# Last block of a fused four-block kernel: eight steps of one head pair regrouped into four steps of two pairs

## The reference

```python
h = _rmsnorm(x, norm_g) * (1 + scale) + shift
c_val, c_gate, c_og, ts, r_og, g_conv, g_rwkv = split(h @ w_in)
# convolution branch: 31 causal taps on each of 1024 channels
u = layernorm(causal_conv(c_val * sigmoid(c_gate), conv_k) + conv_b)
y_conv = (silu(u) * silu(c_og)) @ w_conv_out
# recurrent branch: 16 heads of 64, one state of 64x64 for each head
r, k, v, w_low, a_low = split(ts + mu * (previous(ts) - ts))
for t in tokens:
    sk = state @ kk[t]
    state = state * w[t] - outer(sk, b[t]) + outer(v[t], k[t])
    o[t] = state @ r[t]
o = layernorm_per_head(o) + sum(r * k * r_k) * v
y_rwkv = (o * silu(r_og)) @ w_rwkv_out
m = sigmoid(g_conv) * y_conv + sigmoid(g_rwkv) * y_rwkv
x = x + gate * (m @ w_out);  return _rmsnorm(x, final_g)
```

## Time and profile before

| | us |
|---|---|
| median of 3 runs (1036.30 to 1037.82) | 1036.68 |
| the profiled execution's own time | 1036.78 |
| its span, first to last instruction | 1035.0 |
| TensorE busy in the span | 1002.3 (97%) |
| VectorE busy | 869.7 (84%) |
| ScalarE busy | 604.3 (58%) |

### The profile page before, as it was taken

The page is one execution under the profiler, slowest core; times in us unless marked ns, Lnnn a source line. Parts: engine busy times, 40 slices in busy tenths (PEclk is TensorE's granted clock), DMA queues, the critical chain, the costliest instruction groups (busy, mean ns, idle before and its releaser), DMA issues.

```text
span 1035.0 us, 25000 instructions
## 1 busy us (share of the span) xinstructions
PE 1002.3 (97%) x10690; PEld 932.6 (90%) x10690; DVE 869.7 (84%) x1447; ACT 604.3 (58%) x875; POOL 18.4 (2%) x38
## 2 busy tenths in 40 slices
PE   7999999999999999999999999999999999899997
PEld 6999999999999989989898998889999998789996
DVE  7866699899988886999899897989999999965474
ACT  7755664444446756554444577556657676686443
POOL 2000000000000000000000000000000000000000
PEclk9999999999999999999999999999999999999999
DMA  9662457777554515576775646334323422234531
GB/s 283 214 203 94 152 189 252 230 243 227 199 176 149 164 47 181 200 231 227 241 234 182 203 133 194 109 99 124 122 86 123 125 84 84 84 124 155 170 126 41
DMA packets 136075, 168.26 MB, mean 163 GB/s; under 512 B 3216, under 2 KB 125328, under 8 KB 135728
## 3 DMA queue, kind: packets, MB, share of 16 engines
q1 hardware_dynamic: 132080, 153.44, 46.1%
q0 software_dynamic: 3904, 13.50, 4.0%
HBM read 164.83 MB, written 2.10 MB: 161 GB/s over the span
## 4 chain that ended last, share of the span: by engine, by line
PE 68%; DVE 22%; ACT 6%; issue 2%; DMA 2%; SPq 0%; DVEq 0%; ACTq 0%
PE banks L353 13%; PE banks L318 8%; PE banks L319 7%; PE banks L320 7%; PE banks L355 7%; DVE hf L2652 4%; DVE w_parts L304 3%; DVE w_parts L280 3%; PE banks L655 2%; PE bank L657 2%; PE bank L655 2%; PE banks L657 2%; PE bank L659 2%; PE banks L659 2%; ACT w_parts L275 1%
## 5 line engine op out<-in xcount | busy, mean ns | idle before, releaser
L280 DVE TENSOR_TENSOR w_parts<-raw,w_parts 128x2048 fp32r<-128x2048 f32 x95 | 217.1, 2288 | 27.3 <-ACT w_parts L275 26.8
L353 PE MATMUL banks<-x_parts,w_parts 128*128 128x512 f32 x640 | 227.1, 399 | 0.0
L318 PE MATMUL banks<-x_parts,w_parts 128*128 128x256 f32 x704 | 211.9, 301 | 0.0
L319 PE MATMUL banks<-x_parts,w_parts 128*128 128x256 f32 x736 | 208.3, 283 | 0.0
L320 PE MATMUL banks<-x_parts,w_parts 128*128 128x256 f32 x704 | 199.1, 283 | 0.0
L275 ACT ACTIVATE w_parts<-raw 128x2048 fp32r<-128x2048 f32 x95 | 180.9, 1905 | 3.6 <-PE banks L810 2.1
L355 PE MATMUL banks<-x_parts,w_parts 128*128 128x256 f32 x640 | 179.8, 281 | 0.0
L353 PEld LDWEIGHTS banks<-x_parts,w_parts 128*128 128x128 f32 x640 | 120.3, 188 | 29.0
L319 PEld LDWEIGHTS banks<-x_parts,w_parts 128*128 128x128 f32 x736 | 141.2, 192 | 0.5 <-issue 0.5
L318 PEld LDWEIGHTS banks<-x_parts,w_parts 128*128 128x128 f32 x704 | 134.5, 191 | 7.6 <-issue 0.7
L320 PEld LDWEIGHTS banks<-x_parts,w_parts 128*128 128x128 f32 x704 | 134.8, 192 | 0.0
(11 more groups left out here) (418 smaller groups left out, 2411.6 us busy)
## 6 DMA issues: line engine op xcount, KB each, us to landing
raw<-in_ffn_w_up SPq DMA_DIRECT2D x44, 1024.0 KB, 5.1
raw<-in_w_in SPq DMA_DIRECT2D x36, 1024.0 KB, 5.5
raw<-in_ffn_w_down SPq DMA_DIRECT2D x22, 1024.0 KB, 5.9
big<-in_ada_w_t POOLq DMA_DIRECT2D x24, 512.0 KB, 4.1
raw<-in_gla_w_in SPq DMA_DIRECT2D x11, 1024.0 KB, 5.6
raw<-in_attn_w_qkv SPq DMA_DIRECT2D x6, 1024.0 KB, 4.9
raw<-in_gla_w_out SPq DMA_DIRECT2D x4, 1024.0 KB, 5.5
raw<-in_attn_w_out SPq DMA_DIRECT2D x4, 1024.0 KB, 4.9
```

The costliest lines, as they stand in the source:

```text
L280: eng.tensor_tensor(WL[:, n % RING, :, :], RAW[:, n % RING, :, :], WH[:, n % RING, :, :].bitcast(F32), ALU.subtract).then_inc(w_lo_ready, 1)
L318: nc.tensor.matmul(ps, wh, xh, start=start, stop=False)
L319: nc.tensor.matmul(ps, wh, xl, start=False, stop=False)
L353: nc.tensor.matmul(PS[bank + m].rearrange("p (a t) -> p a t", a=2), WH[:, s, k, ms], XP[:, :, k, :], start=k == 0, stop=False, skip_group_ ...
```

## The change

**Steps of two pairs.** There are now four "duos" of two pairs, and steps -2 to 4 with 13 slots each. Step `s` does the chain of duo `s`, the inverse of duo `s+1`, the fronts of the two pairs of duo `s+2`, and the norms of duo `s-1`. Slots 0 to 2 of the inverse are `scores` and `turned_keys` of the first pair, those of the second pair, and the `seeds`. Slots 3, 5, ..., 11 are `y_part`, slots 4, 6, ..., 12 are `x_part`. Each handles eight chunk parts instead of four, so that VectorE's mask is one operation of 128x512 in place of two of 128x256, and ScalarE's copy is 128x1024 in place of two of 128x512. The chain's copies are 128 wide in place of 64. The number of small matmuls does not change.

**The fronts.** The first pair's front keeps slots 0 to 6, the second pair's goes through slots 6 to 11: ScalarE scales the keys and takes the first sigmoid in slot 6, TensorE sums them in slot 7, VectorE keeps the sums in slot 7, TensorE and ScalarE form the second sigmoid in slot 8, VectorE mixes the keys in slot 8, TensorE sums in slot 9, and so on.

**Remainders in place.** The tiles for two pairs take 24 tiles, for which the remainder part of `w_parts` is used. From the fourth block of the last part to `rout0` the remainder is written over the raw weights (`LO_IN_RAW`), so a load into that slot waits for the matmuls of the block there (`block_done`) and not for its remainder.

**Splits.** The high halves of a block are formed at the last unit of the block two before it and at the first unit of the block before it; the low halves at units 2 and 4 of the block before it.

**Blocks and taps.** Block table as in the diff: 4, 5, 6, 6, 5, 9 blocks in steps -2 to 3, then `cout2`, `cout3` and the last eight. The taps are spread over 114 half slots: the last five slots of step -2 and all of steps -1 to 2. The layer norm of the convolution is in slots 0 to 3 of step 3.

**The end.** `rout_part` is gone. `rout0` is an ordinary block that waits for all pairs in turn (`rwkv_split`). The norms of the last duo are in slots 0 to 2 of step 4, beside `cout2` and `cout3`. The order of splits and mixes on ScalarE and VectorE in the last eight blocks is changed a little.

```diff
 STEP_BLOCKS = {
     -3: _blocks("r0 k0 v0"),
-    -2: _blocks("val0 gate0"),
-    -1: _blocks("r1 k1 v1 val1"),
-    0: _blocks("gate1 val2 rog0 gate2"),
-    1: _blocks("r2 k2 v2 val3"),
-    2: _blocks("gate3 rog1 gr0 gr1"),
-    3: _blocks("r3 k3 v3 gr2"),
-    4: _blocks("rog2 gr3 gc0"),
-    5: _blocks("gc1 gc2"),
-    6: _blocks("rog3 og0 og1 og2 og3"),
-    7: _blocks("gc3 cout0 cout1 cout2 cout3"),
-    8: _blocks("rout0 rout1 rout2 rout3 out0 out1 out2 out3"),
+    -2: _blocks("val0 gate0 k1 r1"),
+    -1: _blocks("v1 val1 gate1 k2 r2"),
+    0: _blocks("v2 val2 gate2 k3 r3 gc0"),
+    1: _blocks("rog0 v3 val3 gate3 gr0 gc1"),
+    2: _blocks("rog1 gr1 gr2 gr3 gc2"),
+    3: _blocks("rog2 gc3 og0 og1 og2 og3 rog3 cout0 cout1"),
+    4: _blocks("cout2 cout3 rout0 rout1 rout2 rout3 out0 out1 out2 out3"),
+DUOS, SLOTS = 4, 13
+LO_IN_RAW = range(N_L3 + 3, N_ROUT + 1)
...
+        def w_lo(n):
+            return (RAW_LO if n in LO_IN_RAW else WL)[:, n % RING, :, :]
...
         def load(sp, n, src, i=0):
-            if n >= RING:
+            if n - RING in LO_IN_RAW:
+                sp.wait_ge(block_done, n - RING + 1)
+            elif n >= RING:
                 sp.wait_ge(w_lo_ready, n - RING + 1 + RING * i)
...
                 for u in range(8):
                     q = (8 * b + u) * last // per
                     put_at(s, q, ("unit", n, u))
-                    if u % 2 == 0:
-                        put_at(s, q, ("hi" if u < 4 else "lo", n + 2, u // 2 % 2))
+                    if u == 0 and n > N_L3 + 3:
+                        put_at(s, q, ("hi", n + 1, 1))
+                    if u in (2, 4) and n > N_L3 + 3:
+                        put_at(s, q, ("lo", n + 1, u // 2 - 1))
+                    if u == 7:
+                        put_at(s, q, ("hi", n + 2, 0))
...
-        TAP_FIRST, TAP_SLOTS = 4, 20 + 6 * 24
+        TAP_FIRST, TAP_SLOTS = 16, 10 + 4 * 2 * SLOTS
...
+            def later_slots(p, q, s, r):
+                if 0 <= p < DUOS:
+                    chain_hop(p, r)
+                for i, (e, c) in enumerate(PARTS):
+                    if 0 <= p < DUOS:
+                        chain_part(p, r, i)
+                    if 0 <= q < DUOS and r % 2:
+                        y_part(q, (r - 3) // 2, e, c)
+                    elif 0 <= q < DUOS:
+                        x_part(q, (r - 4) // 2, e, c)
+                    front_pieces(s + 2, r, i)
+                    norm_pieces(s - 1, s, r, i)
...
              def kk_sums(p, c):
                 if c == 0:
                     pe.wait_ge(sem("kk_squares"), p + 1)
-                    pe.wait_ge(sem("sigmoids_ready"), p + 1)
+                    pe.wait_ge(sem("sigmoids_ready"), 2 * p + (1 if p % 2 else 2))
...
 +            def front(d, r):
...
+                elif r == 6:
+                    keys_scaled(second)
+                    decay_sigmoid(second, T)
+                elif r == 8:
+                    rate_sigmoid(second, 2, T)
+                    kk_root(second)
+                elif r == 10:
+                    decay_exps(second)
...
 +            def front(d, r):
...
+                elif r == 7:
+                    kk_kept(second)
+                elif r == 8:
+                    keys_mixed(second)
+                elif r == 9:
+                    cumulated(second)
+                    bonus(second)
...
-            for j in range(2):
-                rout_part(j, KT - 1)
-            whole(N_ROUT + 2)
-            whole(N_ROUT + 3)
+            for j in range(4):
+                whole(N_ROUT + j)
```

More of the change, by code:

```diff
@@ L1058, in unit @@
                         pe.wait_ge(sem("conv_y_split"), k // 2 + 1)
+                    if n == N_ROUT and m == 0:
+                        pe.wait_ge(sem("rwkv_split"), k + 1)
                     last = three(*operands(n, m, k), k == 0, k == KT - 1)
                 if u == 7:
[L1061 to L1075, removed]
                     last.then_inc(block_done, 1)
@@ new lines, in pre_act_ready, with pre_act_pieces, head_sums @@
+            def pre_act_ready(d):
+                if d == 0:
+                    pe.wait_ge(sem("lora_on_act"), 3)
+                else:
+                    pe.wait_ge(sem("bonus_kept"), 2 * d)
+                if d >= 2:
+                    pe.wait_ge(sem("v_ready"), d - 1)
+            def pre_act_pieces(d, u):
+                decay_piece(2 * d, u, 0)
+                rate_piece(2 * d, u, 6, 0)
+            def head_sums(tile, c, first):
+                for rows in HEADS:
+                    last = nc.tensor.matmul(PS[2][rows, first + c * CH:first + (c + 1) * CH], blk[rows, rows],
+                                            tile[rows, cols64(c)], start=True, stop=True)
+                return last
@@ L1140, in rkrk_sums @@
                     pe.wait_ge(sem("rkrk_ready"), p + 1)
[L1141 to L1143 removed]
+                    if p % 2:
+                        pe.wait_ge(sem("sigmoids_ready"), 2 * p + 2)
+                    elif p // 2 == DUOS - 1:
+                        pe.wait_ge(sem("gn_rstd"), 1)
+                last = head_sums(TMP, c, 0)
@@ new lines, in turn_v, with rhs_at @@
+            def turn_v(d):
+                if d == 0:
+                    pe.wait_ge(sem("mu_ready"), 1)
+                for e, c in PARTS:
+                    for rows in HEADS:
+                        last = nc.tensor.matmul(PS[6][rows, at(e, c)], V_[rows, 2 * d + e, cols64(c)],
+                                                CENTRE[rows, :], start=True, stop=True)
+                last.then_inc(sem("v_turned"), 1)
+            def rhs_at(e):
+                return slice(64 * e, 64 * e + 64)
@@ new lines, in u_product @@
+            def u_product(d, c, e):
+                if e == 0:
+                    pe.wait_ge(sem("rhs_ready"), 4 * d + c + 1)
+                    if c == 0:
+                        pe.wait_ge(sem("inverse_ready"), d + 1)
+                for rows, other in ACROSS:
+                    last = nc.tensor.matmul(PS[3][rows, u_at(e)], XTF[other, at(e, c)], RHS[other, e, :],
+                                            start=e == 0, stop=True, skip_group_check=True)
+                if e:
+                    last.then_inc(sem("u_summed"), 1)
```

933 lines of the change are left out of this document (496 added, 437 removed).

## The result

The changed kernel takes **1084.51 us** (median of 4 runs, 1083.84 to 1086.88) against 1036.49 before (4 runs, 1036.11 to 1037.82): ratio 1.0465, 95% interval 1.0446 to 1.0484. It is 48 us slower, where 5.3 us less were forecast, and outside the range. The profiled execution has a span of 1083.1 us.

A forecast was written before the change was run, and what follows sets the result against it. It took VectorE to bound the last part to about 900 us, TensorE behind it. Step sums, hand-overs and tail gave 406.3 us against 411.6 before, 5.3 less: 1031.5 us, range 1014 to 1045.

The forecast's parts named there:

- (e): Second pair's front, hand-overs inside slots 6 to 9: +5.8 us in steps 0 and 1 each, some +2.5 in step -1.
- (d): Redistributed blocks and taps: work sums by step, VectorE/TensorE, 55.4/46, 58.3/55 and 59.8/56 us in steps -1 to 1.
- Rival 2: ScalarE's turn in slots 6 and 8 is the bound, 9.0 us a step in three steps: about 1044.5, chance 0.24.
- (a): VectorE's masks: two of 256 columns (0.68 us) become one of 512 (0.60), 1.6 us off in all.
- (b): TensorE: 108 slots of steps -1 to 7 become 65; at 0.45 us a change, 10 us saved where TensorE bounds.
- (c): ScalarE: two copies of 0.60 us become one of 1024 columns, about 1.05; nothing on the path.
- (f): Step -2: two fronts one behind the other, little to cover them; VectorE through at 38 us, against 29.6 of work.
- (g): The end: about 1 us of wait in `rout0`, 3 at most; tail from VectorE's last gated sum stays 8.3 us.
- (h): Weight loads: one under way at a time, landing in 5.5 us, 7.6 at most; hidden by 0.5 to 4 us.

The follow-up runs named there:

- e8: Changed kernel with TensorE's sums behind a slot's units, taps begun later and put behind the heads' work, convolution's last hand-over earlier: 1041.93 us.
- e9: Changed kernel, sums still between the parts of the inverse, with taps later and behind the heads' work, convolution's hand-over earlier: 1055.52 us.
- e11: Changed kernel with only the taps moved behind the heads' work in VectorE's order within their slot: 1074.2 us.
- e4: Kernel before the change, without 240 of the 248 convolution taps on VectorE: 1025.99 us.
- e7: Changed kernel with TensorE's sums behind a slot's units, taps beginning 18 half slots later, convolution's last hand-over two half slots earlier: 1043.78 us.
- e12_both: Changed kernel with the front ahead of blocks, splits and taps in hand-over slots, and TensorE's sums behind a slot's units: 1066.09 us.

## Why the prediction was wrong

**The step that failed is (e), with the sum that it was put into.** It priced two hand-overs, the sigmoid that TensorE asks for in slot 7 and the mixed keys in slot 9, at 2.5 us in step -1 and 5.8 in steps 0 and 1, as time of VectorE (9.0 a step as the upper bound), and added that to VectorE's sum of work. As TensorE sees them, these two waits are 1.2, 5.3 and 5.8 us in the three steps: the queue was right, and in steps 0 and 1 so was the size. (The 2.4 us in its slot 6 don't follow from its own figures, 7.8 - 1.6 - 4.2 = 2.0; that is not where it failed.) What it had wrong shows in the account with e8, the same matmuls without these stalls. TensorE's work at full clock is 53.6, 62.8 and 63.8 us. In the changed kernel it is busy 58.7, 65.9 and 68.4, so the clock costs 5.2, 3.0 and 4.7; and it idles the rest, 15.0, 10.1 and 12.4. Together 230.6 for 191.1 in e8, of which 26.5 are waits (37.5 less the 11.0 that e8 has too) and 12.9 clock. Three things were missed:

- *The stalls were set against VectorE's sum, with TensorE's slack as cover.* (d) gave TensorE 46, 55 and 56 us in these steps; e8 shows 7.6 to 7.8 us more in each, so there was little slack, and a stall on TensorE was paid nearly in full. The Trainium skill (Trainium Kernel Development and Optimization, Best Practices) says to judge TensorE by how much of the peak it reaches and by the busy share of its weight loads, not of its matmuls. No run here decides between the two shares: weight loads are busy 92% of step 1 in e8 and 80% in the changed kernel, matmuls 97% and 85%. By the weight loads too, 50.6, 59.7 and 60.6 us in e8, the counts were 4 to 5 short.
- *Only two hand-overs were priced.* They make 12.3 of the 37.5 us. The other 25.2: the pre-activations of slots 6 and 8 (L1114, L1123), which wait for VectorE's kept bonus and kept sums, 8.1; the mask of the scores, 4.6; the root of the norms, in front of the sums of slot 5, 3.9; the first pair's mixed keys there, 2.2; and smaller ones. Most are results of VectorE that stand behind its filler work, whose lag of 1.6 us was taken as given. Moving VectorE's work alone (with one split of ScalarE) gave 29 us (e9), 6 of them at `cout0`; but in step -1 that also took taps out of the step, so the order alone is shown for the 10 us of e11.
- *The clock.* Rival 2's note had the drop, and said that the VectorE-bound steps hide the most of it. They hid nothing; 12.9 us went in three steps, more than the note's ten. The Trainium skill (TensorE: Matmul & The Clock Gate, Part 1) knows two clock states, with the throttled one the default that activity lifts; the trace agrees, 0.22 us a matmul behind the wait of 3.94 and 0.12 later.

The reading that the sum starts from fell as well: the middle of before was called VectorE-bound, and e4 takes 64 us of VectorE's work out of it for 1 us a step.

**Rival 2** named the side and a part of the mechanism, at 1044.5. ScalarE's turn in slots 6 and 8 is only some of the waits, and its price, the upper bound of (e), put these three steps 13 us over the forecast, where 39.6 came.

**(a)** Right: the mask of 512 columns takes 0.60 start to start (853.60 to 854.20).

**(b)** Not borne out. TensorE's steps 1 to 3 without taps in before (e4) are 38.1 us with four blocks of 5.76 and 0.5 of waits: 14.5 for a pair, where the prediction counted 12.7. In e8 step 1, with six blocks and 2.0 of waits, leaves 29.2 for two pairs, 14.6 each, where (d) counted 21.1 for both. Half the slots, the same time: the 0.45 us of a slot change isn't what a slot costs. That is most of what TensorE's counts in (d) lack. It is read from two runs, not tested alone. With it goes one of the two gains, 10 us, on which the forecast rested.

**(c)** Right: 1.02 us for the wide copy.

**(d)** VectorE's sums were right: 29.6, 55.4, 58.3 and 59.8 for steps -2 to 1 are 203.1 us, against 204.8 busy in the changed kernel. TensorE's were 7.6 to 7.8 short in each of steps -1 to 1. The step lengths of e8, 59.5, 65.9 and 65.8, lie within 0.8 us of the forecast's 59, 65.5 and 66.5, but by another sum: in steps 0 and 1 TensorE's 63 to 64 with waits of 2 to 3, beside a VectorE that has some ten more taps a step and is busy 62.3 and 62.8, not VectorE's 58 to 60 and stalls of 6. Agreement of a total proved nothing about its terms.

**(f)** Wrong the other way, 32.9 for 38, but 5 us early for TensorE only: VectorE is busy 22.4 in step -2 where 29.6 were counted, and 61.7 in step -1 for 55.4, so 7 us of its work pass over the border. TensorE's 4.6 us for the mask of the scores at 668.5 are part of the price.

**(g)** Right: `rout0` waits 0.79 us, and that for its remainder and not for the last norms; from VectorE's last gated sum (L3003, at 1074.82) to the end are 8.3 us, as in the earlier trace rows.

**(h)** Wrong in part. ScalarE waited 19.2 us for six loads of `conv_out` and `rwkv_out`, up to 6.0 each; landing takes up to 9.3 where 7.6 was the most. Cutting the loads in half gave 3.6 us from step 3 on. The larger part was a place not looked at: `cout0` waited 3.66 us, with a lowered clock behind it, for `conv_y_lo` of the last two tiles, queued on VectorE behind two half remainders. These wait 3.63 us for ScalarE's split, which comes at 996.90 behind a table load and copies; a late load is 0.52 of that. Moving the hand-over gave 6 us (e7). From step 3 on the part took 141.2, forecast 130.3, 134.2 in e8.

**Step 2** took 55.0 for 50. TensorE is busy 54.3 of it, at full clock: again the count of TensorE, 48.

What stays open: the 5.9 us by which the best variant is over the kernel before. Its weight pipeline, which the memory of the 24 tiles forces, cost 8.8 us by its places alone in before; whether it is these in the new steps wasn't tried. Nor was the new block table tried apart from the steps of two pairs.

## What to carry to other kernels

When a schedule gives up the slot between making a value and asking for it, count for each consumer on TensorE what stands ahead of its producer in the producer's queue, on every engine, and charge the whole wait plus the lowered clock behind it, unless TensorE's own load leaves slack. Look first at moving the question later or the filler work behind the producer (32 and 10 us here), but don't move the question later and the front ahead of the splits at once (e12_both). Where a saving is a number of "changes" times a gap read off one place, check it against a run or stretch in which that engine alone is the bound.

## What the runs showed of the hardware

The lowered clock lasts beyond the stall, while TensorE is busy throughout. In two stretches of the changed kernel at and behind the wait that ends at 837 us (columns as in the first fence):

```profile
836.00:841.00 5.00, 3.77 (x63) 3.68 (x64) 3.65 (x9) 2.30 (x6) 0.00 (x0) 0.55 0.01 3
841.00:846.00 5.00, 5.00 (x124) 4.87 (x125) 4.89 (x13) 0.28 (x1) 0.00 (x0) 0.77 0.00 2
```

In the second TensorE is busy 5.00 of 5.00 us and still gets 0.77 on the mean. That the waits of 10 to 15 us a step took another 3 to 5 us with them in clock was not expected in that size.
